# Gate and up projections of a streaming layer: second Strassen steps in three of seven products

## The chip, the cores and the metric

One core of a Trainium2 chip runs the whole kernel. The metric is the device time in microseconds of one execution; the three runs of the kernel before have a median of 1784.97 us.

## The reference

One inference step of a hybrid encoder layer, all in float32: a combined input projection, latent attention with 8 heads, an RWKV-7 branch with 8 heads, an output projection and a SwiGLU feed-forward part. 1024 prompt rows and 32 sample rows make 1056 token columns. The change lies in the feed-forward part:

```python
def layer_tail(x, attn, rw, attn_out_g, w_out, norm_ffn_g, w_gate, w_up, w_down):
    mix = jnp.concatenate([rmsnorm(attn, attn_out_g), rw], axis=-1)
    h = x + mix @ w_out
    u = rmsnorm(h, norm_ffn_g)
    return h + (jax.nn.silu(u @ w_gate) * (u @ w_up)) @ w_down
```

w_gate and w_up are 1024 x 2816, w_down is 2816 x 1024.

## The kernel before, in words

All of it is in `tail`, which runs after attention. TensorE (PE) holds a 128 x 128 block of weights and streams 264 columns (NW, a quarter of the 1056 tokens) past it; a product of depth KH = 4 adds up four such blocks in a PSUM bank. VectorE is DVE, ScalarE is ACT, GpSimd is POOL, and SP issues the loads.

Gate and up each have 22 blocks of output rows. A **unit** is a pair of them (`pair` and `pair + FH`), and a unit is a 2 x 2 block product, computed with seven half-size products by Strassen's scheme in Winograd's form: P1 = A11 B11, P2 = A12 B21, P3 = S4 B22, P4 = A22 T4, P5 = S1 T1, P6 = S2 T2, P7 = S3 B12. S1 to S4 are sums of weight blocks that POOL makes (lines 2911 to 2925), T1 to T4 are sums of tokens that DVE makes once. A **double** is two units, b = 0 and 1; there are 11 doubles, gate and up in turn, with a mixed one first.

A double has five steps (`STEPS`, line 2516). Steps 0 to 3 are one unit and one column half each (`first_level`, lines 2690 to 2746): P1, P6, P7, P5, P4, P3 of 4 matmuls, 24 in all, in four banks X, Y, Z, W. Step 4 (`second_level`, lines 2748 to 2770) makes P2 of both units together: they share B21, so the two A12 blocks above each other and B21 are again a 2 x 2 block product, with seven products of depth DK = 2, 14 matmuls. The steps use banks 0 to 3 and 4 to 7 in turn. A double is 4 x 24 + 14 = 110 matmuls.

ACT copies the first product out of X (line 2869) and makes tanh. DVE adds bank and copy (lines 3061 to 3065, `front`), which frees the banks for P4 and P3 (semaphores u3_ok and c22_ok), adds again, scales by the row factors rb and multiplies gate by tanh and up by gate (lines 3067 to 3157). Each DVE operation covers 264 columns. POOL makes, for each double, three sums for unit 0, three for unit 1 and one more for each (128 x 512), and then four for the second step (128 x 256, lines 2942 to 2947). SP loads a double's weights in three groups (lines 2567 to 2574), released by the step that last reads the buffers. The queues of all engines keep the order of the program; semaphores join them.

The double's order is followed by the down projection (lines 2778 to 2830), a Strassen product of its own, which begins with sums over hid on DVE (lines 3193 to 3204) and over weights on POOL (lines 2949 to 2968).

Of the kernel before, what the change touches and what calls it, by code (L numbers as in the profile page):

```python
# [2438 lines left out]
def tail(nc, g, io, phase):  # L2439
# [20 lines left out]
    g11 = sb("g11", [P, NW])  # L2460
# [45 lines left out]
    names = """xr_in0 xr_in1 xr_in2 xr_in3 xr_in4 xr_in5 xr_in6 xr_in7 g_in hi_in5 hi_in6 hi_in7 w12_in0 w12_in1 d1_ok d2_ok d3_ok d4_ok dt1_ok dt2_ok dt3_ok dt4_ok fold_ok cs_ok cth_ok lo_in in0 in1 in2 in3 lo_read u_hi1 zero ps_done end_done part_ok h_ok hc_ok sq_ok acc_ok ssq_ps ms_ok r_ok rb_ps rb_ok u_lo u_hi h_st  # L2506
        t1_ok t2_ok t3_ok t4_ok w_in0 w_in1 s1_ok s2_ok s3_ok s4_ok p1_ps p6_ps p7_ps p5_ps x_ps z_ps w_ps
        p1_ok y_done u3_ok c22_ok x_done z_done w_done th11 th22 th21 th12 c_ok hid_ok
        a11_in a12_in a21_in a22_in e1_ok e2_ok e3_ok e4_ok f1_ok f2_ok f3_ok f4_ok q1_ps q6_ps q7_ps q5_ps q4_ps q2_ps q3_ps
        q1_ok q_u2 q_u3 q_c22 q_x q_z q_w res_in y_ok y_st c22_s c11_ok c21_ok c12_ok y_r""".split()  # L2510
# [3 lines left out]
    UNITS = 2 * FH  # L2514
    DOUBLES = [((0, FH - 1), (1, FH - 1))] + [((b, p), (b, p + 1)) for p in range(0, FH - 1, 2) for b in range(2)]
    STEPS = [(d, j) for d in range(FH) for j in range(5)]
    N_STEPS = len(STEPS)
    MIXED, GATES, UPS = 0, 1, 2

    def double_kind(d):  # L2520
        return MIXED if d == 0 else GATES if DOUBLES[d][0][0] == 0 else UPS

    DOWN = [(nh, j) for nh in range(2) for j in range(KH)]

    @block.sync
    def _(sp):
# [23 lines left out]
        def load_unit(u):  # L2550
            (kind, pair), b = DOUBLES[u // 2][u % 2], u % 2
            w = io.w_up if kind else io.w_gate
            sp.dma_start(ab[b][:, 0, 0:KH], w[pair][:, 0:KH]).then_inc(s[f"w_in{b}"], 16)
            sp.dma_start(ab[b][:, 1], w[pair + FH]).then_inc(s[f"w_in{b}"], 16)

        def load_twelve(u):
            (kind, pair), b = DOUBLES[u // 2][u % 2], u % 2
            w = io.w_up if kind else io.w_gate
            sp.dma_start(ab[b][:, 0, KH:], w[pair][:, KH:]).then_inc(s[f"w12_in{b}"], 16)

        for u in range(2):
            load_unit(u)
            load_twelve(u)
# [3 lines left out]
        for d in range(1, FH):  # L2567
            sp.wait_ge(s["w_ps"], 5 * d - 3)
            load_unit(2 * d)
            sp.wait_ge(s["w_ps"], 5 * d - 1)  # L2570
            load_unit(2 * d + 1)
            sp.wait_ge(s["w_ps"], 5 * d)
            load_twelve(2 * d)
            load_twelve(2 * d + 1)
# [4 lines left out]
        for n, (nh, j) in enumerate(DOWN):  # L2579
            if n == 0:  # L2580
                sp.wait_ge(s["w_ps"], N_STEPS - 3)
# [3 lines left out]
                sp.wait_ge(s["w_ps"], N_STEPS - 1)  # L2585
                sp.dma_start(Ahi[:, 0:KH], rows(j + KH)[:, 0:KH]).then_inc(s["lo_in"], 16)
                sp.dma_start(Ahi[:, 2 * KH:FH], rows(j + KH)[:, 2 * KH:FH]).then_inc(s["lo_in"], 16)
                sp.wait_ge(s["w_ps"], N_STEPS)
# [44 lines left out]
    def _(pe):  # L2633
# [47 lines left out]
        def product(bank, left, right, depth, done, first=True):  # L2681
# [3 lines left out]
            ins.then_inc(s[done], 1)  # L2685
            return ins
# [3 lines left out]
        def first_level(it, d, j):  # L2690
            b, nh = j // 2, j % 2
            c = slice(nh * NW, nh * NW + NW)
            X, Y, Z, W = (4 * (it % 2) + i for i in range(4))
            half = lambda t: (lambda k: t[:, k, c])
            A11, _, S3, A22 = (ab[b][:, a, KH * x:KH * x + KH] for a in range(2) for x in range(2))
            u = 2 * d + b
# [12 lines left out]
            if it == 1:
                row_factors()  # L2710
            if it == 0:
                pe.wait_ge(s["s1_ok"], 1)
                pe.wait_ge(s["t1_ok"], 1)
                product(W, left(sw[b][:, 0]), half(T1u), KH, "p5_ps")
            pe.wait_ge(s["s2_ok"], u + 1)
            if it == 0:
                pe.wait_ge(s["t2_ok"], 1)
            if it == 1:
                pe.wait_ge(s["rb_ok"], 1)
            if it >= 2:  # L2720
                pe.wait_ge(s["y_done"], it - 1)
            product(Y, left(sw[b][:, 1]), half(T2u), KH, "p6_ps")
            pe.wait_ge(s["s3_ok"], u + 1)
            if it == 0:
                pe.wait_ge(s["t3_ok"], 1)
            if it == 1:
                pe.wait_ge(s["rb_ok"], 2)
            if it >= 2:
                pe.wait_ge(s["z_done"], it - 1)
            product(Z, left(S3), half(B12u), KH, "p7_ps")  # L2730
            if it:
                pe.wait_ge(s["s1_ok"], u + 1)
                if it == 1:
                    pe.wait_ge(s["rb_ok"], 3)
                if it >= 2:
                    pe.wait_ge(s["w_done"], it - 1)
                product(W, left(sw[b][:, 0]), half(T1u), KH, "p5_ps")
            if it == 0:
                pe.wait_ge(s["t4_ok"], 1)
            pe.wait_ge(s["u3_ok"], it + 1)  # L2740
            product(Z, left(A22), half(T4u), KH, "z_ps", first=False)
            pe.wait_ge(s["s4_ok"], u + 1)
            pe.wait_ge(s["c22_ok"], it + 1)
            product(W, left(sw[b][:, 2]), half(B22u), KH, "w_ps", first=False)
            if it == 0:
                row_sums()

        def second_level(it, d):
            X, Y, Z, W = (4 * (it % 2) + i for i in range(4))
            pe.wait_ge(s["p1_ok"], it - 1)  # L2750
            for b in range(2):
                pe.wait_ge(s[f"w12_in{b}"], 16 * (d + 1))
            product(X, left(a11), left(b11), DK, "p1_ps")
            pe.wait_ge(s["d2_ok"], d + 1)
            pe.wait_ge(s["dt4_ok"], 1)
            pe.wait_ge(s["y_done"], it - 1)
            product(Y, left(d2), left(t2), DK, "p6_ps")
            pe.wait_ge(s["d3_ok"], d + 1)
            pe.wait_ge(s["z_done"], it - 1)
            product(Z, left(a21), left(b12), DK, "p7_ps")  # L2760
            pe.wait_ge(s["d1_ok"], d + 1)
            pe.wait_ge(s["w_done"], it - 1)
            product(W, left(d1), left(t1), DK, "p5_ps")
            pe.wait_ge(s["p1_ok"], it + 1)
            product(X, left(a12), left(b21), DK, "x_ps", first=False)
            pe.wait_ge(s["u3_ok"], it + 1)
            product(Z, left(a22), left(t4), DK, "z_ps", first=False)
            pe.wait_ge(s["d4_ok"], d + 1)
            pe.wait_ge(s["c22_ok"], it + 1)
            product(W, left(d4), left(b22), DK, "w_ps", first=False)  # L2770

        for it, (d, j) in enumerate(STEPS):
            if j < 4:
                first_level(it, d, j)
            else:
                second_level(it, d)

        for n, (nh, j) in enumerate(DOWN):
# [4 lines left out]
            if n == 0:  # L2783
                pe.wait_ge(s["lo_in"], 64)
                pe.wait_ge(s["hid_ok"], 16 * FH - 4)
# [47 lines left out]
    def _(act):  # L2833
# [58 lines left out]
        for n in range(len(DOWN)):  # L2892
            act.wait_ge(s["q1_ps"], n + 1)
            if n == 0:
                act.wait_ge(s["x_done"], FH)
# [479 lines left out]
```

## Time and profile before

| what | value |
|---|---|
| runs of the kernel before | 1782.11, 1784.97, 1786.54 us |
| span of the profiled execution | 1783.9 us (no other time of that execution is given) |
| PE busy | 1724.8 us, 97% |
| DVE, ACT, POOL busy | 1022.5, 416.0, 654.9 us |
| gate and up stage | 950.98 to 1502.95 us |
| down projection | from there to the end |

Times are microseconds from the start of the span. PE is the matmul stream and PEld its weight loads; a float32 matmul of the program stands as two records of PE. Matmul records overlap, so the pitch from one group's start to the next tells more than a record's length. In a timeline a line gives start, length, engine, line of the kernel, operation, output and inputs, shape and number; the bracket gives idle time before it and who ended that.

### The profile page before, as it was taken

The numbers are of one execution on the slowest core, as the hardware profiler recorded it, in microseconds if no ns is written. First come the engines' busy times: TensorE is split into PE (matmuls) and PEld (weight loads), VectorE is DVE, ScalarE is ACT, GpSimd is POOL, SyncE is SP. The second block draws the span as 40 slices with busy tenths as digits, with TensorE's granted clock in tenths as the row PEclk, the third lists the DMA queues.
The fourth block names the chain that finished last, engine by engine and source line by source line (L and its number), as shares of the span: only waits on it lengthen the run. The fifth ranks groups of instructions, "written<-read, shape, count | busy, mean of one in ns | idle before, by whom it ended". The sixth has DMA issues, their size and how long they took to land.

```text
span 1783.9 us, 35048 instructions
## 1 busy us (share of the span) xinstructions
PE 1724.8 (97%) x14688; PEld 1306.3 (73%) x14688; DVE 1022.5 (57%) x1862; ACT 416.0 (23%) x956; POOL 654.9 (37%) x475
## 2 busy tenths in 40 slices
PE   6999999999998998999998999999999999999999
PEld 4566666666665765666766888888888888888887
DVE  3767767767767675665445655545555555526322
ACT  2333243333334233565211110101111010000000
POOL 3563663663653461000151222223332332635332
PEclk9999999999999998999999999999999999999999
DMA  9443243243244314420142111101111012333431
GB/s 359 164 156 110 78 149 110 81 146 110 80 135 116 108 57 105 141 55 1 57 187 97 48 48 48 36 31 47 48 48 48 30 48 78 122 106 106 146 99 60
DMA packets 92754, 169.37 MB, mean 95 GB/s; under 512 B 30043, under 2 KB 63659, under 8 KB 88374
## 3 DMA queue, kind: packets, MB, share of 16 engines
q1 hardware_dynamic: 84134, 119.29, 21.3%
q10 hardware_dynamic: 8464, 47.85, 7.8%
q8 instruction: 117, 1.92, 0.4%
q14 instruction: 39, 0.32, 0.1%
HBM read 136.40 MB, written 23.04 MB: 89 GB/s over the span
## 4 chain that ended last, share of the span: by engine, by line
PE 43%; issue 3%; POOL 2%; SPq 1%; DVE 1%; DMA 1%; ACT 0%; DVEq 0%; POOLq 0%
PE psum L2683 43%; DMA wA<-in_w_gate 1%; POOL u_sum L2959 0%; POOL u_sum L2963 0%; SPq L2529 0%; POOL wA L2954 0%; SPq L2528 0%; POOL wA L2925 0%; POOL wA L2916 0%; POOL wA L2918 0%; DMA wA<-in_w_down 0%; POOL u_sum L2964 0%; SPq L2531 0%; POOL row_ms L2934 0%; SPq L2534 0%
## 5 line engine op out<-in xcount | busy, mean ns | idle before, releaser
L2683 PE MATMUL psum<-mixT,wA 128*128 128x264 f32 x1188 | 285.8, 387 | 0.4 <-DVE mixT L3026 0.4
L2683 PEld LDWEIGHTS psum<-mixT,wA 128*128 128x128 f32 x1188 | 226.6, 191 | 39.8 <-issue 0.8
L535 PE MATMUL psum<-wsl,xt 128*128 128x368 f32 (+2 forms) x716 | 191.8, 443 | 2.9 <-ACT proj L1182 1.7
L2683 PE MATMUL psum<-u_sum,wA 128*128 128x264 f32 x752 | 185.5, 390 | 4.8 <-DVE slot L3063 3.9
L2683 PEld LDWEIGHTS psum<-u_sum,wA 128*128 128x128 f32 x752 | 143.2, 191 | 31.6 <-issue 5.0
L535 PEld LDWEIGHTS psum<-wsl,xt 128*128 128x128 f32 (+1 forms) x716 | 100.6, 169 | 62.3 <-issue 13.1
L2916 POOL TENSOR_TENSOR wA<-wA 128x512 f32<-128x512 f32 x22 | 29.6, 1347 | 294.8 <-DMA wA<-in_w_gate 148.5
L2683 PE MATMUL psum<-hid,wA 128*128 128x264 f32 x506 | 115.1, 386 | 0.6 <-ACT p L2900 0.6
L2683 PE MATMUL psum<-slot,wA 128*128 128x264 f32 x480 | 115.3, 386 | 0.0
L2683 PEld LDWEIGHTS psum<-hid,wA 128*128 128x128 f32 x506 | 96.1, 190 | 17.3 <-issue 1.0
L2683 PEld LDWEIGHTS psum<-slot,wA 128*128 128x128 f32 x480 | 91.2, 190 | 15.6
L535 PE MATMUL psum<-slot,xt 128*128 128x368 f32 (+1 forms) x384 | 97.0, 461 | 5.5 <-DMA slot<-in_w_in 4.7
L1571 POOL TENSOR_TENSOR Ls<-Lraw,con 128x512 f32<-128x512 f32 x45 | 48.7, 1090 | 93.4 <-ACT Lraw L1182 64.9
L2683 PE MATMUL psum<-mixT,u_sum 128*128 128x264 f32 x352 | 79.9, 386 | 1.6 <-POOL u_sum L2964 1.6
L2683 PEld LDWEIGHTS psum<-mixT,u_sum 128*128 128x128 f32 x352 | 66.8, 190 | 13.4 <-POOL u_sum L2964 2.0
L2860 ACT ACTIVATE proj<-slot 128x264 f32<-128x264 f32 x67 | 28.3, 423 | 196.2 <-DVE slot L3080 135.3
L535 PEld LDWEIGHTS psum<-slot,xt 128*128 128x128 f32 (+1 forms) x384 | 51.7, 175 | 30.3 <-issue 7.3
L1535 POOL TENSOR_TENSOR st<-st,con 128x3 f32<-128x3 f32 (+1 forms) x18 | 50.7, 2814 | 60.7 <-DVE st L1733 31.3
L1182 ACT ACTIVATE proj<-psum,rstd 128x368 f32<-128x368 f32 (+1 forms) x72 | 36.8, 512 | 139.0 <-PE psum L535 136.7
L2954 POOL TENSOR_TENSOR wA<-wA 128x1408 f32<-128x1408 f32 x8 | 27.0, 3374 | 104.6 <-DMA wA<-in_w_down 104.6
L2396 DVE TENSOR_REDUCE part<-psum 128x1 f32<-128x347 f32 (+5 forms) x88 | 44.3, 524 | 35.9 <-PE psum L2229 34.9
L2318 ACT ACTIVATE pq<-psum,neg 128x346 f32<-128x346 f32 (+7 forms) x112 | 59.7, 541 | 20.7 <-DVE neg L2399 14.5
(415 smaller groups left out, 3206.9 us busy)
## 6 DMA issues: line engine op xcount, KB each, us to landing
wsl<-in_w_in ACTq DMA_DIRECT2D x18, 1472.0 KB, 6.3
wA<-in_w_down SPq DMA_DIRECT2D x30, 704.0 KB, 4.2
slot<-in_w_in ACTq DMA_DIRECT2D x9, 1472.0 KB, 6.9
mixed<-proj SPq DMA_DIRECT2D x8, 784.0 KB
wA<-in_w_gate SPq DMA_DIRECT2D x22, 256.0 KB, 3.0
wA<-in_w_gate SPq DMA_DIRECT2D x11, 512.0 KB, 4.1
wA<-in_w_up SPq DMA_DIRECT2D x22, 256.0 KB, 3.0
wA<-in_w_up SPq DMA_DIRECT2D x11, 512.0 KB, 4.0
```

The source lines that it names most:

```text
L535: return pe.matmul(out, lhsT, rhs, start=start, stop=stop)
L1182: copy = lambda out, in_, **k: act.activation(out, in_, ACT.Copy, **k)
L1535: tt(out, ms, c_("minus_half")[:, 0:n], ALU.pow).then_inc(s[ok], 1)
L1571: tt(Ls[i % 2][:, :, :], Lraw[:, :, :], bcast(c_("levels")[:, i * 64:(i + 1) * 64], 1, H), ALU.mult).then_inc(s["Ls_ok"], 1)
L2318: act.activation(rows_of(a, t)[:, x:y], pb[n % BANKS][:, 0:y - x], ACT.Exp, bias=neg[:, i % RINGS:i % RINGS + 1], accum_out=sums[:, pair % ...
L2396: dve.tensor_reduce(part[:, r, u:u + 1], src, AX.X, ALU.max).then_inc(s["part_ok"], 1)
L2683: ins = pe.matmul(pb[bank][:, 0:NW], left(k), right(k), start=first and k == 0, stop=k == depth - 1, skip_group_check=not first)
L2860: halved = lambda out, in_: act.activation(out, in_, ACT.Tanh, scale=0.5)
L2916: tt(S1, A21, A22, ALU.add).then_inc(s["s1_ok"], 1)
L2954: tt(Ahi[:, 0:FH], Alo[:, 0:FH], Ahi[:, 0:FH], ALU.subtract).then_inc(s["e3_ok"], 1)
```

## The change

The number of matmuls, the order of the steps, the sums and the loads change; what is computed stays the same. In steps F both column halves of one unit are made together: the two banks of a half-pair are X, X+1 and W, W+1. P6 and P7 are added onto P1 in the bank, ACT copies the values in between, and DVE and ACT work on 528 columns at once. Besides P2, also P4 and (in the first eight doubles) P3 of both units are made in second-level steps S. The order within a double is S4, F0, S2, F1, S3 for doubles 1 to 7 (double 0: F0, S4, F1, S2, S3; the last three have no S3 and make P3 in F). POOL makes twelve small sums for a double, not four, and the weights come in four groups.

```diff
+    def sequence(d):
+        if d == 0:
+            return ((F, 0), (S, 4), (F, 1), (S, 2), (S, 3))
+        if d < LATE_END:
+            return ((S, 4), (F, 0), (S, 2), (F, 1), (S, 3))
+        if d < N_D - 1:
+            return ((S, 4), (F, 0), (S, 2), (F, 1))
+        return ((S, 4), (F, 0), (F, 1), (S, 2))
...
+            if what == F:
+                sp.wait_ge(s["p7_ps"], 2 * n_f[i])
+                load_low(d + 1, n)
+            elif n == 4:
+                sp.wait_ge(s["m3_ps"], n_s[i])
+                sp.wait_ge(s["s1_ok"], 2 * d + 2)
+                load_22(d + 1)
+            elif n == 2:
+                sp.wait_ge(s["m3_ps"], n_s[i])
+                sp.wait_ge(s["s4_ok"], 2 * d + 2)
+                load_12(d + 1)
```

PE, a step F and a step S:

```diff
+            product(X, left(A11), half(B11u, 0), KH)
+            product(X + 1, left(A11), half(B11u, 1), KH, "p1_ps")
...
+            product(W, left(S1), half(T1u, 0), KH)
+            product(W + 1, left(S1), half(T1u, 1), KH, "p5_ps")
...
+            if cut_in_two(d, 2) and not after(d, b, 2):
+                pe.wait_ge(s["c11_ok"], n_added(i))
+            else:
+                pe.wait_ge(s["p1_ok"], n_copied(i))
+            for nh in range(2):
+                product(X + nh, left(S2), half(T2u, nh), KH, "p6_ps", first=False)
+            if not cut_in_two(d, 3):
...
+                product(W, left(S4), half(B22u, 0), KH, first=False)
+                product(W + 1, left(S4), half(B22u, 1), KH, "p3_ps", first=False)
+            if i == 0:
+                pe.wait_ge(s["t3_ok"], 1)
+                row_sums()
+            pe.wait_ge(s["s3_ok"], u + 1)
+            for nh in range(2):
+                pe.wait_ge(s["u2_ok"], 2 * n - 1 + nh)
+                product(X + nh, left(S3), half(B12u, nh), KH, "p7_ps", first=False)
+                if i == 0 and nh == 0:
+                    row_factors()
...
+            product(X, left(a11), left(B[0]), DK, "m1_ps")
...
+            product(Y, left(D[1]), left(T[1]), DK, "m6_ps")
...
+            product(Z, left(a21), left(T[2]), DK, "m7_ps")
...
+            product(W, left(D[0]), left(T[0]), DK, "m5_ps")
+            pe.wait_ge(s["m1_ok"], n)
+            product(X, left(a12), left(B[2]), DK, "m2_ps", first=False)
+            pe.wait_ge(s["v3_ok"], n)
+            product(Z, left(a22), left(T[3]), DK, "m4_ps", first=False)
+            pe.wait_ge(s["d4_ok"], n)
+            pe.wait_ge(s["v22_ok"], n)
+            product(W, left(D[2]), left(B[3]), DK, "m3_ps", first=False)
```

ACT copies P1 (if no step S gave its addend already), P5, and each half of P6, makes tanh of 528 columns, and copies `first_in` out of X in steps S. DVE, where `tt` is tensor_tensor, `stt` scalar_tensor_tensor and `named` waits for its own result:

```diff
+        def scale(x):
+            q, d, b = x
+            h = hid_pair(q, d, b)
+            if gate_unit(d, b):
+                c = q % 10 - 1
+                tt(h, h, rb[:, HT * c:HT * c + HT], ALU.mult).then_inc(s["gr_ok"], 1)
+            else:
+                stt(h, h, 0.5, place(q, d, b), ALU.mult, ALU.mult).then_inc(s["hid_ok"], 1)
...
+        def gates(i):
+            for x in gated_in.get(i, []):
+                n, h = GATED[x], hid_pair(*x)
+                dve.wait_ge(s["th_ok"], n)
+                named(stt(h, th[n % 2], 1.0, h, ALU.add, ALU.mult), "gate_ok", n)
...
+        def second_level(i, d, k):
...
+            named(tt(v2, Y, first_in, ALU.add), "v2_ok", n)
+            dve.wait_ge(s["m7_ps"], n)
+            named(tt(v3, Z, v2, ALU.add), "v3_ok", n)
+            dve.wait_ge(s["m5_ps"], n)
+            if folds(d, k, 0):
+                named(tt(v3, W, v3, ALU.add), "v22_ok", n)
+                fold(o22, v3, i)
...
+            scales(early[:1])
+            if folds(d, k, 1):
+                dve.wait_ge(s["m2_ps"], n)
+                fold(o11, X, i)
+            dve.wait_ge(s["m4_ps"], n)
+            if folds(d, k, 0):
+                named(tt(v3, Z, v2, ALU.add), "v21_ok", n)
+                fold(o21, v3, i)
...
+            scales(early[1:])
+            dve.wait_ge(s["m3_ps"], n)
+            if folds(d, k, 1):
+                named(tt(v2, W, v2, ALU.add), "v12_ok", n)
+                fold(o12, v2, i)
...
+            last = late_scaled.get(i, [])
+            if i < N_STEPS - 1:
+                scales(last)
+                gates(i)
```

POOL, whose `second_sums` is four sums of 128 x 256:

```diff
+        for d in range(N_D):
+            three_sums(d, 0)
+            if d:
+                sums_22(d)
+                three_sums(d, 1)
...
+            fourth_sum(d, 0)
+            fourth_sum(d, 1)
...
+            sums_12(d)
+            sums_4(d)
```

## Rows read from the trace of the kernel before

**Rows 1.** The page, its parts 1 and 4: busy time, and the chain by line.
```profile
PE 1724.8 (97%) x14688; PEld 1306.3 (73%) x14688; DVE 1022.5 (57%) x1862; ACT 416.0 (23%) x956; POOL 654.9 (37%) x475
...
PE psum L2683 43%; DMA wA<-in_w_gate 1%; POOL u_sum L2959 0%; POOL u_sum L2963 0%; SPq L2529 0%; POOL wA L2954 0%; SPq L2528 0%; POOL wA L2925 0%; POOL wA L2916 0%; POOL wA L2918 0%; DMA wA<-in_w_down 0%; POOL u_sum L2964 0%; SPq L2531 0%; POOL row_ms L2934 0%; SPq L2534 0%
```

**Rows 2.** Busy time by stretch, the gate and up stage: PE, PEld, DVE, ACT, POOL, clock, DMA.
```profile
950.98:975.00 24.02, 19.53 (x84) 15.26 (x82) 13.61 (x16) 4.94 (x7) 2.88 (x3) 0.86 0.45 181
975.00:1020.20 45.20, 44.27 (x198) 37.11 (x198) 30.56 (x60) 5.12 (x13) 12.24 (x11) 1.00 0.16 47
1020.20:1502.95 482.75, 482.75 (x2169) 411.70 (x2169) 253.32 (x523) 51.26 (x129) 127.26 (x112) 1.00 0.14 43
```

**Rows 3.** Timeline of PE: the first group of a double and of the next.
```profile
1209.14 1.94 PE L2683 MATMUL psum<-mixT,wA 128*128 128x264 f32 x8
...
1258.12 1.94 PE L2683 MATMUL psum<-mixT,wA 128*128 128x264 f32 x8
```

**Rows 4.** Groups by line and shape, DVE, 1020 to 1503 us.
```profile
L3061 DVE TENSOR_TENSOR slot<-psum,con 128x264 f32<-128x264 f32 x30 | 13.0, 433 | 44.4 <-PE psum L2683 43.9 <-DVE hid L3092 0.3
...
L3128 DVE SCALAR_TENSOR_TENSOR hid<-hid,slot 128x264 f32<-128x264 f32 x5 | 5.1, 1024 | 0.2
```

**Rows 5.** Timeline, start of the stage: two wide operations, and PE's waits.
```profile
951.23 2.62 ACT L2846 ACTIVATE mixT<-hid,g_ffn 128x528 f32<-128x528 f32 x4 [4.22 <-issue]
...
962.96 3.86 PE L2683 MATMUL psum<-u_sum,wA 128*128 128x264 f32 x8 [3.29 <-DVE slot L3063]
...
966.61 3.20 PE L2683 MATMUL psum<-mixT,wA 128*128 128x264 f32 x8
...
969.64 1.99 PE L2671 MATMUL psum<-hid 128*128 128x1 f32 x18
...
986.88 0.71 DVE L3051 TENSOR_TENSOR wo<-mixT 128x528 f32<-128x528 f32 x1
```

**Rows 6.** Timeline across engines, end of an up double: loads, POOL sums and DVE beside them.
```profile
1105.05 0.33 SPq L2553 DMA_DIRECT2D wA<-in_w_gate  x1
...
1109.56 1.26 POOL L2916 TENSOR_TENSOR wA<-wA 128x512 f32<-128x512 f32 x1 [17.46 <-DMA wA<-in_w_gate]
1109.62 1.49 DVE L3128 SCALAR_TENSOR_TENSOR hid<-hid,slot 128x264 f32<-128x264 f32 x1
...
1110.89 1.35 POOL L2918 TENSOR_TENSOR wA<-wA 128x512 f32<-128x512 f32 x1
1111.03 0.42 DVE L3130 TENSOR_TENSOR g<-psum,p 128x264 f32<-128x264 f32 x1
...
1111.28 0.80 SPq L2559 DMA_DIRECT2D wA<-in_w_gate  x2
1111.48 1.05 DVE L3132 SCALAR_TENSOR_TENSOR hid<-hid,g 128x264 f32<-128x264 f32 x1
...
1114.00 2.97 POOL L2925 TENSOR_TENSOR wA<-wA 128x512 f32<-128x512 f32 x2 [0.34 <-DMA wA<-in_w_gate]
```

**Rows 7.** Timeline, end of the stage and start of down: sums on both engines.
```profile
1505.32 3.18 DVE L3198 TENSOR_TENSOR hid<-hid 128x2904 f32<-128x2904 f32 x1
...
1506.68 4.84 POOL L2954 TENSOR_TENSOR wA<-wA 128x1408 f32<-128x1408 f32 x1 [38.49 <-DMA wA<-in_w_down]
...
1508.54 6.02 DVE L3199 TENSOR_TENSOR mixT<-hid 128x2904 f32<-128x2904 f32 x1
...
1525.95 5.16 PE L2683 MATMUL psum<-mixT,u_sum 128*128 128x264 f32 x22 [1.60 <-POOL u_sum L2964]
```

**Rows 8.** Groups by line and shape, POOL, 1020 to 1503 us.
```profile
L2916 POOL TENSOR_TENSOR wA<-wA 128x512 f32<-128x512 f32 x18 | 23.5, 1305 | 263.7 <-DMA wA<-in_w_up 146.3 <-DMA wA<-in_w_gate 117.4
...
L2942 POOL TENSOR_TENSOR con<-wA 128x256 f32<-128x256 f32 x10 | 7.3, 730 | 54.1 <-PE psum L2683 54.1
```

**Rows 9.** Busy time by stretch, an idle stretch of PE and what follows.
```profile
960.00:962.00 2.00, 0.00 (x0) 0.00 (x0) 1.97 (x3) 0.01 (x1) 0.00 (x0) 1.00 1.05 420
964.00:966.00 2.00, 2.00 (x6) 1.59 (x5) 0.57 (x1) 0.00 (x0) 0.00 (x0) 0.50 0.03 8
```

More of the change, by code:

```diff
@@ new lines, in tail, with cut_in_two, after @@
+    STEPS = [(d, what, n) for d in range(N_D) for what, n in sequence(d)]
+    N_STEPS = len(STEPS)
+    at_step = {x: i for i, x in enumerate(STEPS)}
+    n_f = [sum(w == F for _, w, _ in STEPS[:i + 1]) for i in range(N_STEPS)]
+    n_s = [sum(w == S for _, w, _ in STEPS[:i + 1]) for i in range(N_STEPS)]
+    QUADRANT = {2: 11, 3: 12, 4: 21}
+    INNER = {11: 2, 12: 3, 21: 4}
+    def cut_in_two(d, k):
+        return (d, S, k) in at_step
+    def after(d, b, k):
+        return cut_in_two(d, k) and at_step[d, S, k] > at_step[d, F, b]
@@ new lines, in tail, with gate_of @@
+    own_third = lambda i: [x for x in scaled_in.get(i, []) if x == (12, STEPS[i][0], STEPS[i][2]) and STEPS[i][1] == F]
+    late_scaled = {i: [x for x in found if INNER.get(x[0], 0) and after(x[1], x[2], INNER[x[0]])] for i, found in scaled_in.items()}
+    early_scaled = {i: [x for x in found if x not in late_scaled[i] + own_third(i)] for i, found in scaled_in.items()}
+    def gate_of(x):
+        q, d, b = x
+        return (q, d, 0) if d == N_D - 1 else (q, d - 1, b)
+    GATED, n_gated = {}, 0
@@ new lines, in tail @@
+    for i in range(N_STEPS):
+        for x in early_scaled.get(i, []) + own_third(i) + late_scaled.get(i, []):
+            if gate_unit(*x[1:]):
+                n_gated += 1
+                GATED[x] = n_gated
+    N_HID = 4 * 2 * N_D - n_gated
+    n_hid = lambda i: sum(not gate_unit(*x[1:]) for j, found in scaled_in.items() if j <= i for x in found)
+    count = lambda table, i: sum(table(d, b) for d, w, b in STEPS[:i + 1] if w == F)
+    n_copied = lambda i: count(lambda d, b: not (cut_in_two(d, 2) and not after(d, b, 2)), i)
@@ L2523, in tail, with folds @@
+    n_added = lambda i: n_f[i] - n_copied(i)
+    n_whole3 = lambda i: count(lambda d, b: not cut_in_two(d, 3), i)
+    def folds(d, k, b):
+        return after(d, b, k)
+    n_stored = lambda i: sum(not folds(d, k, 1) for d, w, k in STEPS[:i + 1] if w == S)
     DOWN = [(nh, j) for nh in range(2) for j in range(KH)]
@@ L2679, in row_factors, with product @@
                     last.then_inc(s["rb_ps"], 1)
-        def product(bank, left, right, depth, done, first=True):
+        def product(bank, left, right, depth, done=None, first=True):
             for k in range(depth):
@@ L2684, in product, with read_by_now @@
                                 skip_group_check=not first)
-            ins.then_inc(s[done], 1)
-            return ins
+            if done:
+                ins.then_inc(s[done], 1)
         left = lambda w: (lambda k: w[:, k, :])
[L2690 to L2696, printed above, removed]
+        def read_by_now(i):
+            if i < 0:
+                return
+            d, what, n = STEPS[i]
+            if what == F:
+                pe.wait_ge(s["c22_ok"], n_f[i])
+                if after(d, n, 4):
+                    pe.wait_ge(s["x3_ok"], 1)
+            else:
+                pe.wait_ge(s["v12_ok"], n_s[i])
+                if not folds(d, n, 1):
+                    pe.wait_ge(s["cx_ok"], n_stored(i))
@@ L2742, in first_level @@
[L2742 to L2770, printed above, removed]
@@ new lines, in tanh, with all_read, first_level @@
+        def tanh(x):
+            n = GATED[x]
+            act.wait_ge(s["gr_ok"], n)
+            if n > 2:
+                act.wait_ge(s["gate_ok"], n - 2)
+            act.activation(th[n % 2], hid_pair(*x), ACT.Tanh, scale=0.5).then_inc(s["th_ok"], 1)
+        def all_read(i):
+            if i >= 0:
+                act.wait_ge(*((s["c22_ok"], n_f[i]) if STEPS[i][1] == F else (s["v12_ok"], n_s[i])))
+        def first_level(i, d, b):
+            X, W, n = 4 * (i % 2), 4 * (i % 2) + 2, n_f[i]
+            for x in late_scaled.get(i - 1, []):
+                if gate_unit(*x[1:]):
+                    tanh(x)
+            if not (cut_in_two(d, 2) and not after(d, b, 2)):
+                act.wait_ge(s["p1_ps"], n)
+                copy(two(place(11, d, b)), bank_pair(X)).then_inc(s["p1_ok"], 1)
+            if i == 0:
```

595 lines of the change are left out of this document (315 added, 280 removed).

## The prediction, made before the changed kernel ran

> **What bounds the kernel now.** I began with the page: PE is busy 97% of the span, and its line 2683, which holds the gate, up and down products, is 43% of the chain [rows 1]. Then I cut the changed stage into stretches. From 1020 to 1503 us PE is busy for all of 482.75 us, at full clock, and DVE for half of it [rows 2]: nothing but PE's own stream bounds that stretch. The timeline of PE shows its price. One double starts at 1209.14 and the next at 1258.12, 48.98 us for 110 matmuls, 0.445 us each, whether a step is first or second level [rows 3]. So a matmul removed is worth 0.445 us, as long as all banks are read in time. The beginning (950.98 to 1020.20) is looser. Its 282 PE records less 27 small ones for row sums and factors, at half of 0.445, are 56.7 us of 69.2; 12.5 us go to waits, row factors and a low clock.
>
> **What is removed.** A double has 64 matmuls in its F steps and 3 x 14 in its S steps, 106; the last three have 80 + 28 = 108. Eight at 106 and three at 108 are 1172, against 11 x 110 = 1210. 38 fewer at 0.445 are **-16.9 us**. All of them lie on PE's path.
>
> **What the S steps ask of DVE.** A step F lasts 32 x 0.445 = 14.2 us, a step S 6.23. In S, products of two matmuls end every 0.89 us: m1 0.89, m6 1.78, m7 2.67, m5 3.56, m2 4.45, m4 5.34, m3 6.23. m4 starts at 4.45 and waits for v3, the second DVE sum of the step. DVE durations: 264 columns from PSUM take 0.43 us [rows 4], 0.47 with the wait for the result, and 528 take 0.71 [rows 5], of which I take 0.62 where the next doesn't wait. So DVE must be at v2 by 3.5 us into S, or PE stands at m4.
>
> S3 is what stands just before S4 in doubles 1 to 8, with no F between. Its DVE list is the longest: v2, v3, v22, fold, scale (528), fold of o11, v21, fold, scale (528), v12, fold, two late scales (528), and in gate doubles two gates (528). With v2 at 2.05 and v22 done at 4.26 (each 0.27 behind its product), the rest alone takes it to about 9.8 (up) and 11.2 (gate) after S3's start, that is 3.5 and 5.0 into S4. With DVE undisturbed PE would wait about 0 and 1.5 us.
>
> **What POOL does meanwhile.** The timeline shows how the two engines share. A DVE operation with both inputs in SBUF that meets a POOL sum takes 1.49 or 1.05 us, not 0.43, and ends 0.29 us after the POOL sum does; the one with an input in PSUM (line 3130) is not touched; the next POOL sum, 1.35 us instead of 1.26, starts when DVE's is through [rows 6]. The mean of line 3128 is 1024 ns [rows 4]. At the start of down it is the same at larger size: sums of 3.18 us last 6.02 while POOL works beside them [rows 7]. They take turns, an operation each.
>
> SP issues the low weights of the next double's unit 1 at the end of F1, which is S3's start. Before, the issue at 1105.05, with 256 and 512 KB, led to POOL 4.5 us later, and the one at 1111.28 (256 KB) 2.7 us later [rows 6]. For two of 256 KB I take 3.5. Five sums of 1.3 us [rows 8] follow, three and then the two fourth sums, which need only S3's end. They fill 3.5 to 11 us, just where DVE's list is. Taking turns: fold ends at 5.1, scale 6.8, o11 and v21 (PSUM) 7.6, fold 8.2, scale 9.9, v12 10.3, fold 11.3, late scales 12.6, gates 14.05. v3 is then done at 13.5 (up) or 15.0 (gate), while PE would start m4 at 6.23 + 4.45 = 10.7. **PE waits 2.9 us in up and 4.35 us in gate doubles.** S3's end in doubles 1 to 7 gives 4 x 2.9 + 3 x 4.35 = 24.7 us.
>
> Double 0 has S2, S3 and S4 in a row. S2 carries the same list as above, with POOL's sums for S4 beside it: v3 of S3 comes 4.6 us late and v3 of the following S4 2.0 us: **+6.6**. In gate doubles S2 keeps DVE until 7.2 us into F1, where P6 waits for c11_ok from 7.1: 4 x 0.1 = **+0.4**.
>
> **What is hidden.** Twelve small POOL sums instead of four, 8 x 0.73 = 5.8 us a double [rows 8]: those for S2 and S3 run in F0, where DVE's sums read PSUM and the 14.2 us cover them; those for S4 run in F1. Without that cover, 5.8 us a double would be the price. ACT's copies of 528 columns (0.65, [rows 5]) have 2.7 us before P6, those of a half 1.2 us before P7. The loads are the same bytes in eight issues instead of six; each group lands a step or more before its reader, SP has nothing else to do, and its waits hold only later loads of the same buffers. In F, DVE's last two sums end 1.7 us into the next step, before v2 at 2.05.
>
> **Start.** F0 of double 0 now has row_sums before P7, and acc_ok comes behind three token sums more (0.71 each): I get 3.7 us of waiting, against 3.29 before, plus row sums 2.0 [rows 5], 2.5 for the factors and 3.3 of low clock; 11.5 instead of 12.5: **-1**. Between -4 and +4, since the order is new. **End.** DVE's tail behind the last product is some 2.8 us longer, but PE then waits for POOL's sum until 1525.95 [rows 7], which depends on the loads and on taking turns; **0**, between -1.5 and +2.
>
> **Sum.** -16.9 + 24.7 + 6.6 + 0.4 - 1 = **+13.8 us**. Against the span of 1783.9 that is 1797.7; the median of the runs is 1.1 above that span, so I forecast 1798.8. The waits are bounded from below by DVE undisturbed (3 x 1.5 + 2 for double 0 = 6.5 us: net -11) and from above by all five POOL sums in full in front of DVE (3.5 us more at seven places: +38).
>
> **The clock.** PE stood still at 960 to 962 us, a wait of 3.29 us, and after it ran at 0.50 of full clock, 1.2 of 2.4 GHz [rows 5, 9]: 16 records took 6.7 us for 3.6, some 3 us more. The later wait of 1.60 us was followed by full clock [rows 7]. My waits of 2.9 and 4.35 us lie on both sides of 3.29, and m2 may split them. In the sum I take no fall of the clock. The Trainium skill, TensorE: Matmul & The Clock Gate, section HAM oscillation, says that a wait of this sort, repeated, is paid each time with a fall of the clock and a new warm-up. By that rule the sum would be that of rival 3.
>
> **Rivals.**
> 1. *The gain stands* (other side). The place is v3 in the S4 behind S3. If POOL's five sums land outside DVE's list (loads later than 3.5 us, or POOL waiting for another step), or DVE is quicker than my list, v2 is reached within 3.5 to 5 us and PE waits 0 to 1.5. For it: before, every DVE delay was hidden, 482.75 of 482.75 us. Against: before, each S step was followed by steps of 10.7 us. Price 6.5 us: 1784.97 - 11 = 1774; with no wait at all 1767. It decides where all waits together stay under 12.5 us. 0.2.
> 2. *Half of the taking turns.* Waits of 12.5 to 23 us, as when POOL's last two sums come after DVE's scales: 1780 to 1790, about 1785. For it: fourth sums wait for S3's end as DVE's v12 does, and may come second. Against: POOL starts the moment it can [rows 6]. 0.15.
> 3. *The clock falls at the waits.* If each of the nine waits costs 3 us more: 1798.8 + 27 = 1826; at half of them 1812. For: 3.29 us was enough. Against: 1.6 was not, and m2 comes between. 0.2.
> 4. *The change does not do what it says.* The count of matmuls follows from the code, so this can only be if the pitch of a matmul differs in steps S; the old second steps have the same pitch. Under 0.01.
>
> My own case has 0.45, with 1790 to 1806 as its own range.
>
> **How the numbers follow.** A difference of 0.3%, 5.4 us, is about what a measurement of this kernel can tell from none. Faster by more than that is rival 1: 0.2. Within it is rival 2, 0.15. Slower is my case and rival 3, 0.65. The range from 1774 to 1814 leaves out the lower half of rival 1 and the upper half of rival 3.
>
> **What would show it.** In the changed profile the gate and up stage has 2344 PE records at line 2683's kind, with the same pitch. Each S3 and S4 pair should show PE idle before m4, released by DVE's v3, 2 to 5 us long, longer in gate doubles; F0, S2 and F1 should run without gaps. DVE scales and folds beside POOL's 128 x 512 sums should show 1 to 2 us. If those waits are under 1 us I am wrong about taking turns, and the kernel is faster. If records behind them are twice as long, rival 3 holds. Stage length 552 us before: I expect 566, rival 1 has 541, rival 3 up to 590.

## The result and the profile after

| | before | after |
|---|---|---|
| median of the runs | 1783.8 us (4 runs, 1782.1 to 1786.5) | **1821.5 us** (4 runs, 1820.1 to 1822.4) |
| span of the profiled execution | 1783.9 us | 1820.6 us |
| granted TensorE clock, mean over the span | 0.990 | 0.983 |

The changed kernel takes 1.0207 times as long, 95% interval 1.0188 to 1.0226: slower by 37.7 us, and above the upper end of the range that I gave. The page of the changed kernel, its parts 1 and 4:

```profile
PE 1724.9 (95%) x14612; PEld 1300.2 (71%) x14612; DVE 1046.7 (57%) x1703; ACT 444.9 (24%) x987; POOL 738.1 (41%) x551
...
PE 41%; DVE 9%; issue 1%; ACT 0%; DVEq 0%
PE psum L2811 37%; PE psum L2764 4%; DVE hid L3325 2%; DVE hid L3277 1%; DVE hid L3291 1%; DVE hid L3279 1%; DVE hid L3392 0%; DVE mixT L3393 0%; DVE u2c L3339 0%; DVE u2c L3350 0%; DVE u2c L3336 0%; DVE u_sum L3398 0%; PE psum L2799 0%; DVE u2c L3334 0%; DVE u2c L3357 0%
```

PE has 76 records fewer than in [rows 1] (38 matmuls at two records each) and is still busy for 1724.9 us, as before (1724.8). 76 records at 0.2225 us are 16.9, so about as much in slower matmuls has taken their place. And DVE, which had no part in the chain of before, now has 9% of it, by its folds (L3325), scales (L3277, L3279), gates (L3291) and, with under 1% each, the sums v2 and v3 (L3334, L3336).

Waits of PE in the changed kernel: what PE waited for, total us, times, longest. Rows of the earlier stages, whose code the change does not touch, are left out.

```profile
PE psum L2811 <- DVE u2c L3336: 25.7, 9, 4.6
...
PE psum L2799 <- DVE hid L3205: 4.6, 1, 4.6
...
PE psum L2811 <- DVE slot L3409: 3.2, 1, 3.2
PE psum L2811 <- ACT con L3000: 3.2, 3, 1.2
PE psum L2932 <- DVE hid L3279: 3.0, 2, 1.8
...
PE psum L2811 <- DVE hid L3299: 1.9, 4, 1.0
```

Line 3336 is v3. PE waits for it nine times, for 25.7 us in all; beside that ACT's `first_in` copy (line 3000) costs 3.2 and `c11_ok` (line 3299) 1.9. The timeline of PE shows three of the places, in double 0, in an up double and in a gate double:

```profile
1013.45 2.13 PE L2811 MATMUL psum<-hid,wA 128*128 128x264 f32 x4 [4.62 <-DVE u2c L3336]
...
1020.10 1.05 PE L2811 MATMUL psum<-u_sum,wA 128*128 128x264 f32 x4
...
1073.91 1.95 PE L2811 MATMUL psum<-hid,wA 128*128 128x264 f32 x4 [2.74 <-DVE u2c L3336]
...
1123.88 1.16 PE L2811 MATMUL psum<-u_sum,wA 128*128 128x264 f32 x4 [1.17 <-ACT con L3000]
1128.00 1.44 PE L2811 MATMUL psum<-hid,wA 128*128 128x264 f32 x4 [2.96 <-DVE u2c L3336]
1129.23 1.97 PE L2811 MATMUL psum<-u_sum,wo 128*128 128x264 f32 x4
1130.99 4.30 PE L2811 MATMUL psum<-mixT,wA 128*128 128x264 f32 x16
```

Read the durations behind each wait. Four records take 1.05 us at full clock; behind the waits of 4.62 and 2.74 us they take 2.13 and 1.95, about twice that. After the wait of 2.96 us, where the fall comes a little later, eight records begin within 2.99 us instead of 1.78, and sixteen more take 4.30 instead of 3.72: 1.8 us lost. In double 0, sixteen records from 1013.45 to 1020.10 take 6.65 us instead of 3.56: 3.1 lost. The granted clock says the same. Windows over the changed stage, columns as in [rows 2]:

```profile
1025.61:1077.41 51.80, 49.06 (x214) 41.26 (x213) 27.12 (x38) 5.36 (x12) 21.94 (x20) 0.97 0.13 41
1077.41:1130.99 53.58, 49.12 (x213) 40.84 (x212) 29.95 (x42) 10.17 (x20) 21.63 (x20) 0.98 0.13 40
...
1128.00:1131.00 3.00, 3.00 (x9) 2.37 (x10) 0.85 (x2) 0.03 (x1) 0.00 (x0) 0.62 0.00 0
```

A double of 106 matmuls takes 51.80 (up) or 53.58 us (gate), where [rows 3] have 48.98 for 110. The clock, 1.00 throughout this part of the kernel before [rows 2], is 0.97 and 0.98 over a double, and 0.62 in the three microseconds behind a wait: much of that stretch ran at 1.2 instead of 2.4 GHz.

Why v3 is late stands in the timeline across engines, here for S3 of the same gate double. S3 begins on PE at 1113.65:

```profile
1116.50 1.26 POOL L3090 TENSOR_TENSOR wA<-wA 128x512 f32<-128x512 f32 x1 [12.38 <-DMA wA<-in_w_up]
...
1117.06 0.99 DVE L3325 TENSOR_TENSOR hid<-hid,u2c 128x264 f32<-128x264 f32 x1
...
1118.09 1.66 DVE L3277 TENSOR_TENSOR hid<-hid,proj 128x528 f32<-128x528 f32 x1
1119.14 1.74 POOL L3093 TENSOR_TENSOR wA<-wA 128x512 f32<-128x512 f32 x1
1119.67 0.42 DVE L3325 TENSOR_TENSOR hid<-hid,psum 128x264 f32<-128x264 f32 x1
...
1120.85 3.16 POOL L3104 TENSOR_TENSOR wA<-wA 128x512 f32<-128x512 f32 x2
...
1125.57 1.44 DVE L3291 SCALAR_TENSOR_TENSOR hid<-proj,hid 128x528 f32<-128x528 f32 x2
...
1127.52 0.43 DVE L3336 TENSOR_TENSOR u2c<-psum,u2c 128x264 f32<-128x264 f32 x1
```

POOL begins 2.85 us after S3 (I had 3.5) and its five sums last until 1124.01. Beside them a scale of 528 columns takes 1.66 us and not 0.71, a fold 0.99 and not 0.43. The gates end 13.4 us after S3's start (I had 14.05), and only then come v2 and v3 of S4, on which PE has stood since 1125.

**Where the 36.7 us of span went.** The gate and up stage runs from 951.07 to 1534.4, 583.3 us against 552.0, so +31.3. Its matmuls have 1172 x 0.4453 = 521.9 us, 16.9 less. The rest is the start (12.2), waits for v3, for the copy and for `c11_ok` (25.7 + 3.2 + 1.9 = 30.8), the low clock (seven falls at 1.8 and one of 3.1, 15.7) and some 2.7 for restarts behind waits. The low clock is an estimate from the pitch of the records, and the restarts are what is left of the 583.3. What lies behind the stage took 281.0 us before and takes 286.2, +5.2.

### The profile page after: what moved, and what is told of

Its sections match the earlier page's. It is cut to its first block, busy times and chain, and to the rows that moved or that the text cites. A ratio compares the mean times of both kernels' runs of the same rounds, so it can differ in the third digit from the quotient of the medians.

```text
span 1820.6 us, 34845 instructions
## 1 busy us (share of the span) xinstructions
PE 1724.9 (95%) x14612; PEld 1300.2 (71%) x14612; DVE 1046.7 (57%) x1703; ACT 444.9 (24%) x987; POOL 738.1 (41%) x551
## 4 chain that ended last, share of the span: by engine, by line
PE 41%; DVE 9%; issue 1%; ACT 0%; DVEq 0%
PE psum L2811 37%; PE psum L2764 4%; DVE hid L3325 2%; DVE hid L3277 1%; DVE hid L3291 1%; DVE hid L3279 1%; DVE hid L3392 0%; DVE mixT L3393 0%; DVE u2c L3339 0%; DVE u2c L3350 0%; DVE u2c L3336 0%; DVE u_sum L3398 0%; PE psum L2799 0%; DVE u2c L3334 0%; DVE u2c L3357 0%
## 5 line engine op out<-in xcount | busy, mean ns | idle before, releaser
L2811 PE MATMUL psum<-mixT,wA 128*128 128x264 f32 x996 | 237.7, 390 | 0.0
L2811 PEld LDWEIGHTS psum<-mixT,wA 128*128 128x128 f32 x996 | 192.2, 193 | 34.0
L2811 PE MATMUL psum<-hid,wA 128*128 128x264 f32 x614 | 150.1, 398 | 26.3 <-DVE u2c L3336 25.7
L2811 PEld LDWEIGHTS psum<-hid,wA 128*128 128x128 f32 x614 | 118.1, 194 | 50.5 <-DVE u2c L3336 29.5
L2811 PE MATMUL psum<-u_sum,wA 128*128 128x264 f32 x532 | 130.2, 389 | 5.1 <-ACT con L3000 3.2
L2811 PEld LDWEIGHTS psum<-u_sum,wA 128*128 128x128 f32 x532 | 101.1, 191 | 25.0 <-ACT con L3000 4.4
L3308 DVE TENSOR_TENSOR hid<-psum,u2c 128x528 f32<-128x528 f32 x19 | 13.4, 706 | 127.3 <-ACT u2c L3000 94.8
L1535 POOL TENSOR_TENSOR st<-st,con 128x3 f32<-128x3 f32 (+1 forms) x18 | 50.7, 2816 | 60.7 <-DVE st L1733 31.3
L2370 POOL COPY wide<-slot 128x256 f32<-128x256 f32 x16 | 6.4, 401 | 148.4 <-DVE slot L2409 148.4
```

Of the source, the lines that this page charges most:

```text
L1535: tt(out, ms, c_("minus_half")[:, 0:n], ALU.pow).then_inc(s[ok], 1)
```

## The experiments

My theory after the result: DVE's list in S3, stretched by turns with POOL's five sums, makes v3 late, and each long wait also costs a fall of the clock. Its rivals: the list alone is too long, whatever POOL does; or idle time of PE alone makes the loss and the clock none. Each kernel below is the changed kernel with the edit shown; ratios are to the kernel before, beside which the changed kernel has 1.0207.

**POOL's sums later.** POOL makes the three and the two fourth sums of unit 1 only when the next double's S4 has left PE.

```diff
             if d:
                 sums_22(d)
+                pool.wait_ge(s["m3_ps"], n_s[at_step[d, S, 4]])
                 three_sums(d, 1)
```

> The changed kernel, with one wait more on POOL: the three sums of unit 1 (and with them the fourth sums) start only after step S4 of their own double, so that nothing of POOL runs beside DVE's list in S3. Theory A (DVE and POOL take turns on operations with two SBUF inputs, and that makes v3 late; the clock falls behind long waits): PE's waits for v3 fall from 25.7 us to some 6 (about 1.5 in a gate double, 0 in an up double, the rest in double 0), the clock falls hardly anywhere, and the time goes from 1821.5 to about 1786. Rival B (DVE's list is too long by itself, POOL is no cause): waits stay over 20 us and the time within 5 us of 1821. Rival C (the port matters but not the clock): about 1801.

Measured: 1781.4 us (8 runs, 1777.1 to 1788.8), ratio 0.9995, interval 0.9972 to 1.0017. One wait of POOL takes away the whole loss. Waits of PE, with the same earlier stages left out:

```profile
PE psum L2811 <- DVE u2c L3337: 6.1, 4, 2.6
...
PE psum L2811 <- DVE hid L3300: 2.0, 4, 1.0
```

One group of DVE by line and shape from 1025 to 1400 us, first of the changed kernel, then of this one:

```profile
L3279 DVE SCALAR_TENSOR_TENSOR hid<-hid,slot 128x528 f32<-128x528 f32 x4 | 6.6, 1658 | 0.1
```

```profile
L3280 DVE SCALAR_TENSOR_TENSOR hid<-hid,slot 128x528 f32<-128x528 f32 x4 | 2.8, 708 | 0.1
```

The same operation, with the same list in front of v3, is shorter: the scale that always met POOL goes from 1658 ns to 708. The waits left are 1.17 us in gate doubles and none in up doubles. That is the "about 0 and 1.5 us" of DVE undisturbed, so the rival of the list alone falls. The waits for v3, the copy and line 3299 are shorter by 30.8 - 8.1 = 22.7 us, the end's wait by 1.9 (3.2 to 1.3); of the falls of the clock one is left, 1.8 us behind a wait of 2.60 in double 0, so 15.7 - 1.8 = 13.9 are saved. That makes 38.5. In the traces the stage is 38.1 us shorter (545.3 against 583.3) and what lies behind it 2.9, 41.0 in all; the medians lie 40.1 apart, and the spans 45.3, of which 4.3 stand ahead of the stage, where both kernels run the same code. Where POOL's sums went shows that they had cover elsewhere:

```profile
1111.08 1.16 PE L2811 MATMUL psum<-hid,wA 128*128 128x264 f32 x4 [1.17 <-DVE u2c L3337]
...
1113.21 1.27 POOL L3090 TENSOR_TENSOR wA<-wA 128x512 f32<-128x512 f32 x1 [22.79 <-PE psum L2811]
1113.70 3.03 DVE L3292 SCALAR_TENSOR_TENSOR hid<-proj,hid 128x528 f32<-128x528 f32 x2
```

DVE and POOL still take turns (two gates last 3.03 us and not 1.44), but in F0, where nobody waits. The Trainium skill, SBUF — State Buffer, section "SBUF: two separate sides", describes the mechanism: the two engines share a pair of ports, which is held for a whole instruction by whichever starts first, and a DVE operation takes part if both its inputs are in SBUF. The traces agree: `hid<-hid,psum` kept its 0.42 us beside a POOL sum of 1.74, `hid<-hid,proj` did not keep its 0.71.

**DVE's scales and gates later.** In a step S followed by a step S, late scales and gates are put behind v22 of the following step.

```diff
+            while put_off:
+                put_off.pop(0)()
             early = early_scaled.get(i, [])
...
-            if i < N_STEPS - 1:
+            if i < N_STEPS - 1 and STEPS[i + 1][1] == S:
+                put_off.append(lambda: (scales(last), gates(i)))
+            elif i < N_STEPS - 1:
                 scales(last)
```

> The changed kernel, with DVE's late scales and gates of a step S that is followed by another S put behind the third sum of that next step; nothing else differs. Theory A: v2 and v3 of S4 wait only for DVE's work up to the last fold of S3, which POOL's sums push to 5.1 us into S4: about 1.6 us of waiting at each of the seven places, the same in up and gate doubles, under 1 in double 0, and no fall of the clock: about 1790. Rival B (what is late is not DVE's order but ACT's copy or the sums over weights): within 5 us of 1821.

Measured: 1793.6 us (8 runs, 1788.2 to 1802.3), ratio 1.0056, interval 1.0033 to 1.0079. Waits of PE, and then its timeline in an up and in a gate double:

```profile
PE psum L2811 <- DVE u2c L3337: 8.4, 8, 1.7
PE psum L2811 <- ACT con L3000: 6.6, 4, 3.2
```

```profile
1065.96 1.16 PE L2811 MATMUL psum<-hid,wA 128*128 128x264 f32 x4 [1.66 <-DVE u2c L3337]
1066.95 1.05 PE L2811 MATMUL psum<-u_sum,wo 128*128 128x264 f32 x4
...
1114.31 1.16 PE L2811 MATMUL psum<-u_sum,wA 128*128 128x264 f32 x4 [1.22 <-ACT con L3000]
1115.70 1.16 PE L2811 MATMUL psum<-hid,wA 128*128 128x264 f32 x4 [0.24 <-DVE u2c L3337]
```

This shows two things. A wait of 1.66 us is not followed by a low clock (1.05 us for four records), where 2.74 us was. And when DVE is out of the way, the next late thing is ACT: its copy of `first_in` stands behind its tanh, 1.22 us in a gate double and 3.2 in double 0. Waits fall by 30.8 - 16.9 = 13.9 us. One fall of 1.6 us is left, in double 0, so the falls account for another 14.1, and the two together for 28.0. The stage is 27.3 us shorter in the trace, what lies behind it 2.9, and the medians lie 27.9 apart.

**PE kept busy while it waits.** In front of the wait for v3, in steps S behind a step S, PE does extra matmuls whose results nobody reads: 10 in double 0, 2 in double 1, 6 in the others.

```diff
+            if i and STEPS[i - 1][1] == S:
+                for _ in range(10 if d == 0 and k == 3 else 2 if d == 1 else 6):
+                    pe.matmul(pb[4 * ((i - 1) % 2) + 1][:, NW:512], a12[:, 0, :], B[2][:, 0, 0:512 - NW], start=True, stop=True,
+                              skip_group_check=True)
             pe.wait_ge(s["v3_ok"], n)
```

> The changed kernel, with PE given extra matmuls (248 columns, into unused columns of a bank that is not in use, results dropped) before it waits for v3 in a step S behind a step S: 10 in double 0, 2 in double 1, 6 in each of the others. They fill the wait and add work. If the clock's fall behind the waits costs 13 to 18 us (theory A), the time goes down, by that much less some 3 us where a fill is longer than its wait: about 1807, with a granted clock of 0.99 in the profile. If the clock costs nothing (rival), the time stays at 1821.5 or rises by up to 5 us.

Measured: 1811.9 us (2 runs, 1810.5 and 1813.3), ratio 1.0159, interval 1.0114 to 1.0204; the span is 11.9 us below that of the changed kernel. Timeline of PE in the gate double, and windows of the stage:

```profile
1119.54 1.16 PE L2811 MATMUL psum<-u_sum,wA 128*128 128x264 f32 x4 [1.29 <-ACT con L3004]
1120.54 2.67 PE L2907 MATMUL psum<-u_sum,wA 128*128 128x248 f32 x12
1123.66 1.16 PE L2811 MATMUL psum<-hid,wA 128*128 128x264 f32 x4 [0.45 <-DVE u2c L3340]
1124.65 1.05 PE L2811 MATMUL psum<-u_sum,wo 128*128 128x264 f32 x4
```

```profile
983.00:1024.00 41.00, 39.44 (x178) 33.34 (x177) 38.37 (x49) 7.84 (x15) 26.09 (x22) 1.00 0.13 40
1024.00:1300.00 276.00, 271.07 (x1213) 229.40 (x1212) 147.50 (x207) 39.35 (x83) 117.15 (x110) 1.00 0.14 42
```

m4 starts 4.12 us behind m2, just as in the changed kernel (1119.54 to 1123.66 here, 1123.88 to 1128.00 there), yet the kernel is faster, since all behind m4 runs at full clock: 1.00 in both windows. That prices the clock apart from the waits: 9.6 us in the medians, 11.9 in the spans, 12.5 in the stage alone (570.9 against 583.3), and about 2 more for what fills and waits are longer here over all nine places, where I had counted 15.7 from the records. Behind the stage this run is 1.7 us longer; the clock fell there twice, behind waits of 1.77 and 2.52 us, which it did not do in the changed kernel. So some 12 to 15 us of the loss are clock, and the rival in which it costs nothing falls.

**S3 in one double only.** `LATE_END` from 8 to 1: doubles 1 to 7 make P3 in F, so no S4 stands behind an S3 there, at the price of 14 matmuls.

```diff
-    LATE_END = N_D - 3
+    LATE_END = 1
```

> The changed kernel with S3 in double 0 alone; doubles 1 to 9 make P3 in their F steps as the last ones do. 14 matmuls more (1186 instead of 1172: +6.2 us), but no step S follows a step S from double 2 on. Theory A: no waits for v3 there, so 1821.5 + 6 - 20 (waits) - 13 (clock) = about 1794; the wait in double 0 and the end of the stage (5 us) stay. If S steps in themselves are what is dear (rival), waits appear behind S2 and S4 as well and the time is over 1810.

Measured: 1791.6 us (4 runs, 1789.5 to 1795.2), ratio 1.0037, interval 1.0014 to 1.0061. Waits of PE:

```profile
PE psum L2811 <- DVE u2c L3336: 6.6, 2, 4.6
...
PE psum L2811 <- DVE hid L3299: 4.4, 4, 1.2
```

With the seven places gone only the waits of double 0 and the S4 behind it are left, and the loss goes from 2.07% to 0.37%. But this kernel has 24 matmuls fewer than the one before, 10.7 us, and shows nothing of them: these waits (6.6, and a fall of 1.6 behind the first), line 3299 (4.4) and the end (287.8 us behind the stage, 6.8 more than before, with two falls of the clock in it) come to 19.4. That leaves +8.7; the medians show +7.8. No S2 or S4 that stands behind an F step waits for v3, so steps S in themselves are not what is dear.

**Both of the first two edits.**

> Both cures at once: POOL's sums of unit 1 after step S4, and DVE's late scales and gates behind the third sum of the next step S. Theory A: each cure took one of the two things that made v3 late, so what is left is 0 from double 1 on, c11_ok in gate doubles (2 us) and 2 us in double 0: 1783.8 - 16.9 (matmuls) + 4 (these waits) + 5 (end of the stage) = about 1776. Rival (the two cures take away the same waits): no better than the POOL one alone, 1781.

Measured: 1777.0 us (6 runs, 1770.8 to 1779.8), ratio 0.9955, interval 0.9938 to 0.9972. No wait for v3 or for the copy is left in the view of PE's waits; what it has of the stage is the start and line 3300:

```profile
PE psum L2799 <- DVE hid L3206: 4.6, 1, 4.6
...
PE psum L2811 <- DVE hid L3300: 1.4, 2, 1.1
```

The two edits do not take away the same waits: the stage lasts 536.4 us, 8.9 less than with POOL's sums later alone. The medians show 4.4 of it, and the spans of the two traces none (1775.6 and 1775.3). Half of the difference is behind the stage, 287.8 us against 283.3, where the clock fell twice, the rest ahead of the stage. The timeline of PE behind the stage, first of this kernel, then of the changed one:

```profile
1495.65 0.71 PE L2932 MATMUL psum<-hid,wA 128*128 128x264 f32 x2 [1.77 <-DVE hid L3280]
1496.94 11.72 PE L2811 MATMUL psum<-hid,wA 128*128 128x264 f32 x44 [0.57 <-ACT con L3073]
...
1520.85 5.49 PE L2811 MATMUL psum<-slot,wA 128*128 128x264 f32 x16 [2.40 <-DVE slot L3415]
```

```profile
1567.53 3.80 PE L2811 MATMUL psum<-slot,wA 128*128 128x264 f32 x16 [3.23 <-DVE slot L3409]
```

The same 16 records take 5.49 us behind a wait of 2.40, and 3.80 behind one of 3.23, where the granted clock stays 1.00. The 44 records behind the wait of 1.77 take 11.72 us; behind the same wait of the changed kernel they take 10.05. So the length of a wait alone does not say whether the clock falls.

**The ends alone.** In the changed kernel, DVE makes the last squares ahead of the sums for T4, and the row means ahead of the four token sums, so that row sums are not waited for; and POOL's first down sum waits until DVE's last scale is done.

```diff
+        add_squares(KD - 2)
         for k in (6, 7):
             weighted(k, slice(0, HT), "u_hi")
+        add_squares(KD - 1)
         dve.wait_ge(s["u_hi"], KH)
...
             if i == 0:
                 row_means()
+                dve.wait_ge(s["t4_ok"], 1)
+                token_sums_of(4, 0, 4)
...
             pool.wait_ge(s["a21_in"], 16 * n + 16)
+            if n == 0:
+                pool.wait_ge(s["hid_ok"], N_HID)
```

> The changed kernel with only the two orders at the start and at the end of the stage; the middle is untouched. Theory A: the waits of the middle stay (25 us for v3, clock falls there), the start gains 6 us, the end 3: 1821.5 - 9 = about 1812. Rival (both only move a wait to the next reader): within 3 us of 1821.5.

Measured: 1818.2 us (2 runs, 1814.3 and 1822.1), ratio 1.0194, interval 1.0165 to 1.0222; span 1812.5. In the changed kernel the first S4 starts 26.4 us after the stage, here 19.9: PE waits 0.51 us for row sums and not 4.62. So the start gave 6.5 us. The end gave nothing: what lies behind the stage takes 286.7 us, and 286.2 in the changed kernel. PE's wait for line 3409 (3.2 us), which no fall of the clock followed, gave way to one of 3.2 for POOL's sum at line 3175, and the 22 records behind that take 8.16 us and not the 5.16 of [rows 7]:

```profile
1551.52 8.16 PE L2811 MATMUL psum<-mixT,u_sum 128*128 128x264 f32 x22 [3.15 <-POOL u_sum L3175]
```

The span is 8.1 us lower, the median 3.4 from two runs that lie 8 apart, less than the 9 that I expected.

**All together.** The two edits, the ends, and POOL's sums of unit 0 of the next double only after S2 of the current one.

```diff
         for d in range(N_D):
+            if d:
+                pool.wait_ge(s["m3_ps"], n_s[at_step[d - 1, S, 2]])
             three_sums(d, 0)
```

> Both cures, and three orders more: POOL's sums of unit 0 after step S2 (against the waits for c11_ok), POOL's first sum of the down projection after DVE's last product of hid, and at the start the squares ahead of T4 and of the token sums, with the row means between them. Theory A: 1776, less 2 for c11_ok, less 3 at the end, less 6 at the start (row sums four us earlier and no fall of the clock in front of them) = about 1765. Rival: the sums put off are late for their own readers, and a new wait takes their place: 1776 or more.

Measured: 1769.4 us (5 runs, 1768.8 to 1771.1), ratio 0.9923, interval 0.9910 to 0.9937: 14 us below the kernel before, 52 below the changed one, and 4 above what I expected. The stage in one window:

```profile
950.70:1481.70 531.00, 527.80 (x2372) 448.89 (x2370) 284.69 (x436) 88.95 (x179) 214.48 (x199) 1.00 0.15 51
```

The stage lasts 531.0 us, 21.0 less than before: the 16.9 of the matmuls, and 4.1 that the start gains after what small waits cost (PE is busy for 527.80 of the 531.00). About 4 of the 21 are given back behind the stage, 285.3 us against 281.0, where POOL's held sums now come late. PE waits 3.14 us for the sum at line 3178, and behind that a group of 22 records that takes 6.78 us and not the 5.16 of [rows 7]. I did not try to move that wait further.

## Why the prediction was wrong where it was

**The matmuls**: right. 76 records fewer, pitch unchanged (16 records in 3.56 us wherever the clock is full).

**The waits for v3, and taking turns**: right. I had 24.7 us at seven places, 6.6 in double 0 and 0.4 for `c11_ok`, 31.7 in all; measured were 25.7 + 3.2 + 1.9 = 30.8. The parts moved a little against each other: gate doubles wait 2.96 for v3 and 1.17 for ACT's copy, together 4.13 against 4.35; up doubles 2.74 to 2.95 against 2.9; S3 of double 0 waits 4.62 and the S4 behind it 0.80, where I had 4.6 and 2.0. Line 3299 cost 1.9 where I had 0.4. That the total came within 1 us is partly luck, since these misses cancel. I had called ACT's copies hidden; that they hold for F steps and not in S behind S was missed, and it did not count because v3 was later still. Moving POOL's five sums alone made the waits 0 and 1.17 us, so the turns are shown to be their cause.

**The clock**: the step that failed. "In the sum I take no fall of the clock" was the wrong end. Eight of the nine waits, 2.7 to 4.6 us long, were followed by half clock. My reason for the zero was that 2.9 lies under the 3.29 us seen before [rows 5, 9] and over the 1.60 [rows 7]; between two rows, the one 0.4 us away was the nearer, and I took the other. For the gate doubles (4.35) and double 0 (4.6), which lie above 3.29, there was no row for a zero at all, only the thought that m2 may split the wait. It did split it in gate doubles, into 1.17 and 2.96, and the clock fell all the same. The price per fall was off too, to the other side: rival 3 gave 3 us, from [rows 9], and measured are 1.8 at seven places and 3.1 in double 0. In all it is 12 to 15 us by the kernel with PE kept busy, 15.7 by the pitch of the records. What I cited from the Trainium skill, TensorE: Matmul & The Clock Gate, section HAM oscillation, is told there of a kernel with waits of some 3 to 5 us, each of which is paid with a fall. This trace agrees for the wait of 4.62, goes further, with falls behind the seven of 2.74 to 2.96, and has one of 3.23, in the down projection, with none. Rival 3 was thus the mechanism that took place: it said up to 590 us for the stage, measured 583.3, and I had expected 566.

**The start**: the size was nearly right (12.2 us, I had 11.5, before 12.5). That another order of DVE's list would shorten it I did not see; the one above gives 6.5 us back.

**The end**: the second term that was mis-sized. I took 0, between -1.5 and +2; it was +5.2 us. The timeline across engines, at the end of the stage:

```profile
1535.82 4.69 PE L2932 MATMUL psum<-hid,wA 128*128 128x264 f32 x20 [1.24 <-DVE hid L3279]
...
1538.11 3.56 POOL L3163 TENSOR_TENSOR wA<-wA 128x1408 f32<-128x1408 f32 x1 [38.15 <-DMA wA<-in_w_down]
1538.75 3.48 DVE L3279 SCALAR_TENSOR_TENSOR hid<-hid,con 128x528 f32<-128x528 f32 x1
...
1542.28 0.71 PE L2932 MATMUL psum<-hid,wA 128*128 128x264 f32 x2 [1.77 <-DVE hid L3279]
```

DVE's last scale, 0.71 us of work, ran into POOL's first down sum and took 3.48; PE stood for it 1.77 us. DVE's large sums over hid, which began 2.4 us behind the stage before [rows 7], now began 7.9 behind it, at 1542.26. I had added up DVE's tail and named the turns, and did not put the one into the other. That this is what the 5.2 us are is read from the trace and not shown by an experiment: in the kernel with the ends alone the scale takes 0.71 us again, and another sum of POOL's and a fall of the clock took what that freed.

In one line: -16.9 - 0.3 (start) + 30.8 + 2.7 + 15.7 is +32 for the stage, measured +31.3, and +5.2 behind it; the difference between my +13.8 and the 36.7 of the spans is, but for what rounding leaves, the clock (15.7), the end (5.2) and the restarts behind waits (2.7).

## What to carry to other kernels

When a change saves work on the engine that bounds, list for every other engine what lies in front of the operand that is due first, and lay POOL's SBUF sums beside DVE's: an operation of DVE with both inputs in SBUF lasted here until 0.3 to 0.6 us after the end of the POOL sum that it met. One wait that holds POOL back to a step where DVE's work is not urgent was worth 40 us here, and no new wait of PE came with it. Price a wait of TensorE like those here, 2.4 us and more, as the wait and a fall of its clock, expect now and then a fall behind a shorter one, and if the wait can't be removed, try to fill it.

## What the hardware showed that I had not expected

- The granted clock fell behind waits of PE that are shorter than the 3.29 us of before, but not by their length alone. From the start of the stage on, the nine traces have 32 waits of 2.40 us or more, and a fall within 3 us behind 31 of them; the one without is the 3.23 us in the changed kernel's down projection. Of twelve waits of 1.60 to 1.95 us three were followed by a fall: the same wait of 1.77 us at the same place, with a fall in three kernels and without one in three others. What decides it no run here shows.
- The price of a fall differs: 1.8 us behind the waits of 2.7 to 3.0, 3.1 behind the wait of 4.62 in double 0, and 1.6 behind the same wait of 4.62 in the kernel with S3 in one double.
- Matmuls that compute nothing useful made the kernel 9.6 us faster. The intervals of the two ratios, 1.0114 to 1.0204 and 1.0188 to 1.0226, overlap slightly; the spans (1808.7 against 1820.6), the length of the stage (570.9 against 583.3) and the windows at clock 1.00 point the same way.
- A DVE operation of 0.71 us took 3.48 beside one POOL sum of 1408 columns (3.56 us), and 1.66 beside one of 512 columns (1.34 us): the price went with the length of the sum that it met.
